# One more gate chunk by seven products in front of the attention, and GpSimd's adds in pairs

## The chip, the cores and the metric

The kernel runs on one core of a Trainium2 chip. The metric is the device time of one execution in microseconds (us); the times of several runs are given as their median. The core has TensorE (PE, with its weight loads as PEld), VectorE (DVE), ScalarE (ACT), GpSimd (POOL) and SyncE (SP), each with an instruction queue of its own, and DMA queues that SP, ACT and POOL feed.

## What is computed

The reference is two transformer blocks in a row over 512 tokens of width 1024, in float32. The change lies in the first one:

```python
proj = h @ w_in                                   # q_a k_a v_a z_a q_b k_b v_b z_b f g
y_a = stick_breaking(q_a, k_a, v_a); y_a = (y_a * silu(z_a)) @ w_o_sb
y_b = forgetting_attention(q_b, k_b, v_b, cumsum(log_sigmoid(f + b_forget)))
y_b = (y_b * silu(z_b)) @ w_o_fox
gates = sigmoid(g + b_gate)                       # 2048 columns: 1024 for y_a, 1024 for y_b
merged = gates[0] * y_a + gates[1] * y_b
x = rmsnorm(x + gate * (merged @ w_out))
```

The second block (pooling, a recurrent mixer, differential attention, memory attention and a convolutional feed-forward layer of width 2816) follows; its feed-forward weights come into this change through their sums alone.

## The kernel before

Activations lie as columns: 128 partitions by 512 tokens for each tile of 128 features. Every large product is done in three matmuls on float32r parts: a value is split in a "high" part (rounded by ScalarE) and a "low" part (value minus high, by VectorE or GpSimd), and high*high, high*low and low*high are added in PSUM.

Weights come as a stream of 1 MB chunks of 256 columns (two tiles). SyncE loads them into three slots, each as soon as TensorE has used the chunk three before it. ScalarE rounds a chunk (`split_weights`, L1508), GpSimd makes its low half in four pieces (`low_weights`, L3310), and TensorE uses it. All of this is an order written out by hand for each engine's queue.

The first block goes through these stages:

- **Seven products in front** (`EARLY_TILES`, `early_product`). For 11 chunks, each chunk's product with h is done as 2x2 blocks by seven half-size products in place of eight: 84 matmuls of 128x256 a chunk. VectorE makes the sums of weights and the low halves here. Gate chunks 6 and 7 (tiles 12 to 15) are the last two of them; they land in the place of the later `vb` tiles (`GATES_AT`), and are stored to memory and loaded again after the attention.
- **First attention ("a", stick-breaking)**, 16 steps in `stick_step`, with the plain products of `vb` and `zb` between them on TensorE; then **second attention ("b", forgetting)**, 16 steps in `fox_step`, with gate tiles 0 to 7 between them. A step of the second one does, on VectorE, the bias subtraction (L2659), two scalings of the weights of the step before (L2671), and the mask of the next step (L2636); TensorE transposes the scaled weights one step later (L669).
- Gate tiles 8 and 9 go with the last steps, and tiles 10 and 11 follow the attention as plain products: 24 matmuls of 128x512 a tile.
- **Output products** "oa" and "ob" (8 tiles each, 12 matmuls of 128x512 a tile) of the gated attention outputs, whose low halves (`gated_lo`) VectorE makes right behind the attention. VectorE multiplies each tile with its gate (L2693, L2698), adds the two (L2701), ScalarE rounds the sum (`merged_hi`, L1535), VectorE subtracts (`merged_lo`, L2360).
- **The w_out product**, 8 tiles of 24 matmuls, each over the eight `merged` slices in order.

In the shadow of the attention two sets of sums of the feed-forward weights ("up sums" and "down sums") are made in device memory: ScalarE's queue copies a first matrix, and GpSimd's queue adds a second one by accumulating DMAs (`add`: eight for the up sums, then eight for the down sums, 704 KB each, behind chosen weight chunks). ScalarE's `later_copies` then copies these sums on; it is called in the loop over the eight `merged` tiles, and before its first copy it waits for all of those adds:

```python
for m in range(KD):
    act.wait_ge(sem("merged_raw"), m + 1)
    high(merged_hi[m], merged_raw[:, m, :], sem("merged_hi"))
    if m % 2 == 0:
        later_copies(S2, S1, m // 2, 2)   # m == 0: waits for 8 + 8 adds to have landed
    if m % 4 == 3:
        split_weights()
```

Of the kernel before, what the change touches and what calls it, by code (L numbers as in the profile page):

```python
# [7 lines left out]
F32 = mybir.dt.float32  # L8
# [78 lines left out]
EARLY_FIRST = 11  # L87
EARLY_TILES = (("qa", 1), ("ka", 0), ("ka", 1), ("za", 0), ("za", 1), ("qb", 0), ("qb", 1), ("kb", 0), ("kb", 1), ("g", 6), ("g", 7))
EARLY = len(EARLY_TILES)
Z_FIRST, EARLY_G = EARLY_TILES.index(("za", 0)), 12  # L90
EARLY_STEPS = [[(c, f) for c, fs in ((i, (P1, R5)), (i - 1, (Q4, P3)), (i, (R7, P6, P2))) if 0 <= c < EARLY for f in fs]
# [93 lines left out]
def build(nc, x_in, mem_in, params_in, consts_in, ada_in, stream_in, with_f_in, down_in, up_in, out, x2_kept, kx_kept, vx_kept, nF_kept, gates_kept, sums_kept, up_sums):  # L185
    with ExitStack() as ctx:
# [156 lines left out]
        GATES_AT = 10240  # L343
        gates = [at(512 * m if m < EARLY_G else GATES_AT + 512 * (m - EARLY_G), T) for m in range(16)]
        merged_raw, merged_lo = at(16384, 8, T), at_r("merged_low", 16384, 8, T)
# [207 lines left out]
        def early_tile(e, half, side):  # L553
            key, c = EARLY_TILES[e]
            if key == "g":
                return gates[2 * c + half][:, TH * side:TH * (side + 1)]
            to = {"qa": qa, "ka": ka, "za": gated["a"], "qb": qb, "kb": kb}[key]
            return to[:, 2 * c + half, TH * side:TH * (side + 1)]
# [99 lines left out]
        def _(pe):  # L658
# [313 lines left out]
            for i in range(2 * N + LAG + 1):  # L972
                if i == 1:
                    pe.wait_ge(sem("product_moved"), MOVED0)
                if i < N:
                    head_scores("a", i, qa, ka, masks[:, 1, :])
                elif i < 2 * N:
                    head_scores("b", i - N, qb, kb, None)
                n = i - LAG
                if n == N:  # L980
                    side(i)
                if 0 <= n < N:
                    head_turns("a", n, SLOTS_A, sem("stick_w"))
                elif N <= n < 2 * N:
                    head_turns("b", n - N, SLOTS_B, sem("fox_w"))
                if i < 2 * N:
                    if n != N:
                        side(i)
                elif i < 2 * N + LAG:
                    if i == 2 * N:  # L990
                        M.use([0, 1, 2, 3])
                    project("g", 1, KD, h, T, first=SIDE_G + i - 2 * N)
                n = i - LAG - 1
                if 0 <= n < N:
                    head_values("a", n, va)
                elif n >= N:
                    if n == N:
                        for m in range(4):
                            F.wait_out(pe, ("vb", m))
                    head_values("b", n - N, vb)  # L1000
# [475 lines left out]
        def _(act):  # L1476
# [269 lines left out]
            for n, (e, f) in enumerate(EARLY_SEQ):  # L1746
                if n and EARLY_SEQ[n - 1][1] in (P1, P6):
                    early_keep(*EARLY_SEQ[n - 1])
                if f == R7:
                    early_sum_high(e + 1, R5)  # L1750
                    early_split(e + 1)
                    if e == 1:
                        act.wait_ge(sem("nF_ready"), 1)
                        act.dma_start(nF_kept, f_work[0:HEADS, 1, :]).then_inc(sem("nF_stored"), 16)
                    if e - 2 in (Z_FIRST, Z_FIRST + 1):
                        for m in range(2):
                            silu("a", 2 * (e - 2 - Z_FIRST) + m)
                elif f == P2:
                    early_sum_high(e + 1, P6)
                    if e == 0:  # L1760
                        act.wait_ge(sem("keys_kept"), 32)
                    early_sum_high(e, P3)
# [44 lines left out]
            def stick_step(i):  # L1807

                if i == 1:
                    act.wait_ge(sem("product_moved"), MOVED0)  # L1810
                    act.dma_start(gates_kept, at(GATES_AT, 4 * T)).then_inc(sem("keys_kept"), 16)
                if i == 2:
                    act.wait_ge(sem("nF_stored"), 16)
                    act.wait_ge(sem("keys_kept"), 48)
                if i % 2 == 0 and 2 <= i <= N:
# [43 lines left out]
            def fox_step(i):  # L1859
# [15 lines left out]
                if i in (5, 9):  # L1875
                    pair = i // 4 + 1
                    M2.wait_out(act, ("b", NB * (pair - 1) - 1))
                    act.dma_start(nF_bc[pair % 2], nF_kept[2 * pair:2 * pair + 2, :].partition_broadcast(P))\
                        .then_inc(sem(f"nF{pair % 2}_loaded"), 16)
                if i % 2 == 0 and 2 <= i <= N:  # L1880
                    gate_inverse(i // 2 - 1)
# [17 lines left out]
            for m in range(4):  # L1899
                gated_high(4 + m)  # L1900
            act.dma_start(at(GATES_AT, 4 * T), gates_kept).then_inc(sem("keys_kept"), 16)
            for m in range(SIDE_G, EARLY_G):
                gate_out(m)
                gate_inverse(m)
            act.wait_ge(sem("keys_kept"), 64)
            for m in range(EARLY_G, 16):
                link(nc.scalar.activation(gates[m], gates[m], ACT.Exp, scale=-1.0, bias=npar("b_gate", m)))
                inverse(gates[m]).then_inc(sem("gates"), 1)

            for _ in range(2):  # L1910
                split_weights()
            for m in range(KD):
# [423 lines left out]
        def _(dve):  # L2336
# [167 lines left out]
            def early_out(n):  # L2504
# [6 lines left out]
                o = early_bank(e, f)  # L2511
                if f == P2:
                    early_moves(stt(early_tile(e, 0, 0), o, by, k1, ALU.mult, ALU.add))
                    if e < EARLY - 1:
# [115 lines left out]


            def mask_block(i):

                b = block_of("b", i)
                v = nF_bc[i // NB % 2][:, :, P * b:P * (b + 1)]
                tt(v, v, con("mask_incl").unsqueeze(1).broadcast_to([P, 2, P]), ALU.add).then_inc(sem("block_masked"), 1)  # L2636

            def fox_step(i):
# [6 lines left out]
                if i < N:  # L2645
# [11 lines left out]
                    for hh in range(2):  # L2657
# [3 lines left out]
                                                             small[:, c:c + 1])  # L2661
                    ins.then_inc(M2.out(("b", i)), 1)
                n = i - 1
                if 0 <= n < N:
# [20 lines left out]

            for m in range(8):
                dve.wait_ge(sem("gated_hi"), m + 1)
                low(gated_lo[:, m, :], gated_raw[:, m, :], gated_hi[m], sem("gated_split"))

# [608 lines left out]
        def _(pool):  # L3298
# [44 lines left out]
            for c in range(4, 8):  # L3343
                low_weights(vb + 5 + c, vb + 6 + c)
                add(S1, A22, 2, c)
                add(S3, A11, 2, c)
            low_weights(vb + 13, mixers + 1)
            with_sums(mixers + 1, mixers + HI, S2, A11, 3, 0)
# [178 lines left out]
def lay_stream(a):  # L3527
# [3 lines left out]
    for i in (2, 0, 1, 3, 4, 5, 6, 7):  # L3531
        columns_ = lay_chunks(w_in[:, 512 * i:512 * (i + 1)], 256)
        parts.append(columns_[::-1] if i == 2 else columns_)
        if i == 5:
            parts.append(by_gates[EARLY_G // 2:])
    parts.append(by_gates[:EARLY_G // 2])
    parts.append(lay_chunks(np.asarray(a["w_o_sb"])[0], 512))
# [61 lines left out]
```

## Time and profile before

| | |
|---|---|
| time, median of 3 runs | 1241.11 us (1240.2 to 1241.29) |
| the profiled execution | 1237.92 us, its span 1236.1 us |
| granted TensorE clock | 1.000 |
| TensorE busy | 1211.6 us, 98% of the span |
| VectorE, ScalarE, GpSimd busy | 855.9, 653.7, 429.7 us |

The span is the time from the first to the last instruction of the profiled execution. Matmuls overlap in the engine, so a busy TensorE is not one at its peak. All times in the rows below count from the start of that span.

### The profile page before, as it was taken

The numbers are of one execution on the slowest core, as the hardware profiler recorded it, in microseconds if no ns is written. First come the engines' busy times: TensorE is split into PE (matmuls) and PEld (weight loads), VectorE is DVE, ScalarE is ACT, GpSimd is POOL, SyncE is SP. The second block draws the span as 40 slices with busy tenths as digits, with TensorE's granted clock in tenths as the row PEclk, the third lists the DMA queues.
The fourth block names the chain that finished last, engine by engine and source line by source line (L and its number), as shares of the span: only waits on it lengthen the run. The fifth ranks groups of instructions, "written<-read, shape, count | busy, mean of one in ns | idle before, by whom it ended". The sixth has DMA issues, their size and how long they took to land.

```text
span 1236.1 us, 22894 instructions
## 1 busy us (share of the span) xinstructions
PE 1211.6 (98%) x9270; PEld 1039.7 (84%) x9270; DVE 855.9 (69%) x1342; ACT 653.7 (53%) x1028; POOL 429.7 (35%) x330
## 2 busy tenths in 40 slices
PE   6999999999999999999998999999999999999999
PEld 5798999876767888777787768788878999999999
DVE  4299897789653275596647758356568888878974
ACT  6555463777765534463456554454335555556452
POOL 5562000422333745455343035540555223333000
PEclk9999999999999999999999999999999999999999
DMA  9953332666976974766321018851533555556554
GB/s 388 362 187 139 117 110 96 241 220 215 265 202 165 251 271 172 238 152 156 92 104 37 4 69 312 258 136 34 143 123 101 164 183 186 187 171 211 187 187 141
DMA packets 42182, 215.53 MB, mean 174 GB/s; under 512 B 5080, under 2 KB 5208, under 8 KB 28128
## 3 DMA queue, kind: packets, MB, share of 16 engines
q1 hardware_dynamic: 34272, 140.74, 32.1%
q0 software_dynamic: 4608, 28.31, 12.1%
q10 hardware_dynamic: 3200, 45.04, 9.7%
q8 instruction: 74, 1.21, 0.4%
q14 instruction: 28, 0.23, 0.1%
HBM read 206.72 MB, written 63.98 MB: 219 GB/s over the span
## 4 chain that ended last, share of the span: by engine, by line
PE 85%; DVE 9%; ACT 3%; issue 2%; POOL 1%; DMA 0%; ACTq 0%; SPq 0%; DVEq 0%; POOLq 0%
PE banks L662 83%; PE banks L669 2%; DVE arena L2619 1%; DVE arena L2616 1%; DVE arena L2621 1%; DVE h_low L2360 1%; ACT weights_high L1508 0%; DMA arena<-in_mem 0%; POOL arena L3369 0%; DVE arena L2450 0%; DVE weights_low L2360 0%; ACT arena L1562 0%; DVE sums L2356 0%; DVE gact_low L2360 0%; DVE arena L3261 0%
## 5 line engine op out<-in xcount | busy, mean ns | idle before, releaser
L3310 POOL TENSOR_TENSOR weights_low<-weights,weights_high 128x512 fp32r<-128x512 f32 (+1 forms) x216 | 309.2, 1460 | 495.7 <-ACT weights_high L1508 495.7
L662 PE MATMUL banks<-h_high_low,weights_high 128*128 128x512 f32 (+1 forms) x696 | 243.5, 350 | 0.4 <-DVE h_low L2360 0.3
L662 PE MATMUL banks<-h_high_low,weights_low 128*128 128x512 f32 (+1 forms) x696 | 236.1, 339 | 0.0
L662 PE MATMUL banks<-h_low,weights_high 128*128 128x512 f32 (+1 forms) x696 | 236.1, 339 | 0.0
L1508 ACT ACTIVATE weights_high<-weights 128x2048 fp32r<-128x2048 f32 (+2 forms) x86 | 127.0, 1489 | 63.6 <-PE banks L662 58.4
L662 PEld LDWEIGHTS banks<-h_high_low,weights_high 128*128 128x128 f32 x696 | 131.3, 189 | 19.3 <-issue 3.0
L662 PEld LDWEIGHTS banks<-h_low,weights_high 128*128 128x128 f32 x696 | 131.3, 189 | 16.5 <-issue 2.4
L662 PEld LDWEIGHTS banks<-h_high_low,weights_low 128*128 128x128 f32 x696 | 131.2, 189 | 16.0
L662 PE MATMUL banks<-arena 64*64 64x64 f32 (+6 forms) x1800 | 116.7, 263 | 1.4 <-POOL arena L3369 0.7
L662 PEld LDWEIGHTS banks<-arena 64*64 64x64 f32 (+3 forms) x1800 | 85.0, 147 | 23.8 <-issue 16.7
L3388 POOL TENSOR_TENSOR weights_low<-weights,weights_high 128x512 fp32r<-128x512 f32 x32 | 48.5, 1537 | 112.6 <-ACT weights_high L1520 112.6
L1520 ACT ACTIVATE weights_high<-weights 128x1024 fp32r<-128x1024 f32 x56 | 59.0, 1057 | 35.2 <-PE banks L662 34.1
L2360 DVE TENSOR_TENSOR weights_low<-weights,weights_high 128x1024 fp32r<-128x1024 f32 (+1 forms) x47 | 60.5, 1287 | 13.9 <-ACT weights_high L1520 11.8
L1562 ACT ACTIVATE arena<-banks 128x512 f32<-128x512 f32 (+4 forms) x78 | 39.3, 513 | 37.8 <-PE banks L669 32.3
L1545 ACT ACTIVATE sums<-xres 128x512 f32<-128x512 f32 x32 | 20.2, 632 | 69.4 <-DVE xres L2713 38.5
L662 PE MATMUL banks<-weights_high,h_high_low 128*128 128x256 f32 (+1 forms) x192 | 55.5, 289 | 0.8 <-POOL weights_low L3310 0.6
L662 PE MATMUL banks<-token_sum_high,weights_low 128*128 128x256 f32 x192 | 54.3, 283 | 0.0
L662 PE MATMUL banks<-weights_high,h_low 128*128 128x256 f32 (+1 forms) x192 | 54.3, 283 | 0.0
L662 PE MATMUL banks<-weights_low,h_high_low 128*128 128x256 f32 (+1 forms) x192 | 54.3, 283 | 0.0
L662 PE MATMUL banks<-token_sum_low,weights_high 128*128 128x256 f32 x192 | 54.2, 282 | 0.0
L662 PE MATMUL banks<-token_sum_high,weights_high 128*128 128x256 f32 x192 | 54.0, 281 | 0.0
L662 PE MATMUL banks<-t_high,weights_low 128*128 128x256 f32 x187 | 52.6, 281 | 0.0
(463 smaller groups left out, 3288.1 us busy)
## 6 DMA issues: line engine op xcount, KB each, us to landing
weights<-in_stream SPq DMA_DIRECT2D x66, 1024.0 KB, 6.0
up_sums<-in_up POOLq DMA_DIRECT2D x16, 1024.0 KB, 9.6
weights<-up_sums SPq DMA_DIRECT2D x64, 256.0 KB, 2.8
weights<-in_up SPq DMA_DIRECT2D x48, 256.0 KB, 2.9
sums_kept<-in_down POOLq DMA_DIRECT2D x16, 704.0 KB, 7.4
arena<-in_ada SPq DMA_DIRECT2D x8, 1024.0 KB, 12.1
weights<-sums_kept SPq DMA_DIRECT2D x9, 704.0 KB, 4.1
sums_kept<-in_down ACTq DMA_DIRECT2D x8, 704.0 KB, 5.9
```

The costliest lines, as they stand in the source:

```text
L662: ins = nc.tensor.matmul(o, lhsT, rhs, start=start, stop=stop, skip_group_check=skip)
L669: ins = nc.tensor.transpose(o, i, ident[0:rows, 0:rows])
L1508: nc.scalar.activation(hi_of(c)[:, cols], raw_of(c)[:, cols], ACT.Copy)\
L1520: nc.scalar.activation(pair_hi(q), pair_raw(q), ACT.Copy).then_inc(sem("piece_hi"), 1)
L1545: nc.scalar.activation(SQ[n][i % 2][:, 0:width], src[:, k, 0:width], ACT.Square)\
L1562: nc.scalar.activation(dst, s_, ACT.Copy).then_inc(ring_.out(key), 1)
L2360: return tt(lo, raw, hi.bitcast(F32), ALU.subtract).then_inc(done, 1)
L2616: link(stt(w, o[:, :, 0:end], 0.0, w, ALU.max, ALU.add))
L2619: ins = nc.vector.tensor_tensor_scan(v, ones(end), v, 0.0, ALU.mult, ALU.add)
L2621: tt(w, o[:, :, 0:end], w, ALU.subtract).then_inc(M2.out(("a", i)), 1)
L3310: nc.gpsimd.tensor_tensor(lo_of(c)[:, cols], raw_of(c)[:, cols], hi_of(c)[:, cols].bitcast(F32), ALU.subtract).then_inc(sem("weights_split ...
L3388: nc.gpsimd.tensor_tensor(piece_of(pair_lo, n), piece_of(pair_raw, n), piece_of(pair_hi, n).bitcast(F32), ALU.subtract).then_inc(sem("piec ...
```

## The change

- `EARLY_TILES` gets a twelfth chunk, gate chunk 5 (tiles 10 and 11), after the `za` chunks. Its result lands at 8192, the place of the later `kb` tiles; ScalarE's queue stores it to `gates_kept` two chunks later, VectorE waits for that store before it writes the first `kb` chunk, and ScalarE's queue loads it to tiles 10 and 11 in step 4 of the second attention.
- Tiles 12 to 15 are copied to the SBUF tile `sums` in place of device memory, and ScalarE's exponentials read them there; the reload after the attention goes.
- The plain products of tiles 10 and 11 go, so "oa" follows the attention directly. The first four subtractions for `gated_lo` (`gated_split`) move into steps 5, 9, 13 and 17 of the second attention. One of ScalarE's chunk splits moves between the exponentials of tiles 13 and 14.
- TensorE waits for the last of the early moves at step 2 of the first attention in place of step 1, and tiles 8 and 9 take banks 2 and 3 first.
- GpSimd's adds to the down sums go four behind one chunk and four behind the next ("oa"'s two) in place of two behind each of four. The adds to the up sums stay behind the same steps.

```diff
-EARLY_TILES = (("qa", 1), ("ka", 0), ("ka", 1), ("za", 0), ("za", 1), ("qb", 0), ... ("g", 6), ("g", 7))
+EARLY_TILES = (("qa", 1), ("ka", 0), ("ka", 1), ("za", 0), ("za", 1), ("g", 5), ("qb", 0), ("qb", 1),
+               ("kb", 0), ("kb", 1), ("g", 6), ("g", 7))
-Z_FIRST, EARLY_G = EARLY_TILES.index(("za", 0)), 12
+Z_FIRST, EARLY_G = EARLY_TILES.index(("za", 0)), 10
...
+        early_gates = {5: at(8192, 2, T), 6: at(GATES_AT, 2, T), 7: at(GATES_AT + 2 * T, 2, T)}
...
             for i in range(2 * N + LAG + 1):                       # TensorE, attention
-                if i == 1:
+                if i == LAG:
                     pe.wait_ge(sem("product_moved"), MOVED0)
...
                     if i == 2 * N:
-                        M.use([0, 1, 2, 3])
+                        M.use([2, 3, 0, 1])
                     project("g", 1, KD, h, T, first=SIDE_G + i - 2 * N)
...
                     early_split(e + 1)                             # ScalarE, early stage
+                    if e >= 2 and EARLY_TILES[e - 2] == ("g", 5):
+                        act.wait_ge(sem("product_moved"), early_moved(e - 2, C12))
+                        act.dma_start(gates_kept, at(8192, 2 * T)).then_inc(sem("keys_kept"), 16)
...
                 if i == 1:                                         # ScalarE, first attention
                     act.wait_ge(sem("product_moved"), MOVED0)
-                    act.dma_start(gates_kept, at(GATES_AT, 4 * T)).then_inc(sem("keys_kept"), 16)
+                    act.dma_start(sums.rearrange("p a b -> p (a b)"), at(GATES_AT, 4 * T)).then_inc(sem("keys_kept"), 16)
                 if i == 2:
                     act.wait_ge(sem("nF_stored"), 16)
-                    act.wait_ge(sem("keys_kept"), 48)
+                    act.wait_ge(sem("keys_kept"), 64)
...
+                if i == 4:                                         # ScalarE, second attention
+                    act.dma_start(at(512 * EARLY_G, 2 * T), gates_kept).then_inc(sem("keys_kept"), 16)
...
-            act.dma_start(at(GATES_AT, 4 * T), gates_kept).then_inc(sem("keys_kept"), 16)
             for m in range(SIDE_G, EARLY_G):
                 gate_out(m)
                 gate_inverse(m)
-            act.wait_ge(sem("keys_kept"), 64)
+            act.wait_ge(sem("keys_kept"), 80)
             for m in range(EARLY_G, 16):
-                link(nc.scalar.activation(gates[m], gates[m], ACT.Exp, scale=-1.0, bias=npar("b_gate", m)))
+                if m == 14:
+                    split_weights()
+                src = gates[m] if m < 12 else sums[:, m - 12, :]
+                link(nc.scalar.activation(gates[m], src, ACT.Exp, scale=-1.0, bias=npar("b_gate", m)))
                 inverse(gates[m]).then_inc(sem("gates"), 1)
-            for _ in range(2):
-                split_weights()
+            split_weights()
...
                 if f == P2:                                        # VectorE, early stage
+                    if EARLY_TILES[e] == ("kb", 0):
+                        dve.wait_ge(sem("keys_kept"), 48)
...
+            def gated_split(m):
+                dve.wait_ge(sem("gated_hi"), m + 1)
+                low(gated_lo[:, m, :], gated_raw[:, m, :], gated_hi[m], sem("gated_split"))
...
                     ins.then_inc(M2.out(("b", i)), 1)              # VectorE, fox_step, after L2659
+                if i % 4 == 1 and 5 <= i <= N + 1:
+                    gated_split(i // 4 - 1)
                 n = i - 1
...
-            for m in range(8):
-                dve.wait_ge(sem("gated_hi"), m + 1)
-                low(gated_lo[:, m, :], gated_raw[:, m, :], gated_hi[m], sem("gated_split"))
+            for m in range(4, 8):
+                gated_split(m)
...
             for c in range(4, 8):                                  # GpSimd, adds to the down sums
-                low_weights(vb + 5 + c, vb + 6 + c)
+                if c % 2 == 0:
+                    low_weights(vb + 7 + c // 2, vb + 8 + c // 2)
                 add(S1, A22, 2, c)
                 add(S3, A11, 2, c)
-            low_weights(vb + 13, mixers + 1)
+            low_weights(vb + 11, mixers + 1)
```

The order of the chunks in the stream is changed to match, and `gates_kept` shrinks to two tiles.

## Rows read from the trace of the kernel before

**Rows 1.** The page, part 1: busy us (share), instructions.

```profile
PE 1211.6 (98%) x9270; PEld 1039.7 (84%) x9270; DVE 855.9 (69%) x1342; ACT 653.7 (53%) x1028; POOL 429.7 (35%) x330
```

**Rows 2.** Windows of TensorE: us, PE busy (x), PEclk, DMA share, GB/s.

```profile
111.75:221.83 110.08, 109.99 (x927) 1.00 0.31 110
394.77:406.13 11.36, 11.36 (x51) 1.00 1.00 290
406.13:450.92 44.79, 44.79 (x193) 1.00 0.92 262
```

**Rows 3.** Waits of TensorE, 205 to 330 us: total, times, longest.

```profile
PE banks L662 <- DVE arena L2621: 0.2, 1, 0.2
PE banks L669 <- ACT arena L1831: 0.2, 1, 0.2
```

**Rows 4.** Waits of TensorE, 330 to 520 us.

```profile
PE banks L662 <- DVE h_low L2360: 0.3, 1, 0.3
```

**Rows 5.** Timeline of ScalarE, step 2 of the first attention: start, us, what.

```profile
229.69 0.60 ACT L1562 ACTIVATE arena<-banks 128x512 f32<-128x512 f32 x1 [1.81 <-DMA gates_kept<-arena]
```

**Rows 6.** Timeline of VectorE, GpSimd and TensorE, step 5 of the second attention.

```profile
327.79 0.56 DVE L2659 CUSTOM_DVE_ANT_0 arena<-banks,arena 128x384 f32<-128x384 f32 x1
328.05 5.56 POOL L3310 TENSOR_TENSOR weights_low<-weights,weights_high 128x512 fp32r<-128x512 f32 x4 [13.17 <-ACT weights_high L1508]
...
328.47 2.59 DVE L2671 TENSOR_SCALAR arena<-arena,small 128x512 f32<-128x512 f32 x2
...
332.19 0.66 PE L669 MATMUL banks<-consts,arena 128*128 128x128 f32 x4
```

**Rows 7.** Timeline of VectorE, step 9 of the second attention.

```profile
348.23 2.59 DVE L2671 TENSOR_SCALAR arena<-arena,small 128x512 f32<-128x512 f32 x2
```

**Rows 8.** Timeline of VectorE in the merged loop.

```profile
432.25 1.64 DVE L2701 TENSOR_TENSOR arena<-arena 128x512 f32<-128x512 f32 x1
...
439.95 0.69 DVE L2360 TENSOR_TENSOR merged_low<-arena,merged_high_a 128x512 fp32r<-128x512 f32 x1 [1.18 <-ACT merged_high_a L1535]
...
441.89 0.69 DVE L2360 TENSOR_TENSOR merged_low<-arena,merged_high_a 128x512 fp32r<-128x512 f32 x1
...
452.95 1.47 DVE L2360 TENSOR_TENSOR merged_low<-arena,merged_high_b 128x512 fp32r<-128x512 f32 x2
```

**Rows 9.** Timeline of ScalarE around its first later copy (ACTq: its sequencer issues).

```profile
433.93 0.64 ACT L1535 ACTIVATE merged_high_a<-arena 128x512 fp32r<-128x512 f32 x1 [3.20 <-DVE arena L2701]
438.74 0.50 ACTq L1769 DMA_DIRECT2D up_sums<-up_sums  x1
439.29 0.63 ACT L1535 ACTIVATE merged_high_a<-arena 128x512 fp32r<-128x512 f32 x1 [4.73 <-DVE arena L2701]
```

**Rows 10.** Timeline of GpSimd: two of its four pairs of adds.

```profile
392.36 1.65 POOL L3328 DMA_DIRECT2D sums_kept<-in_down  x2
...
406.94 1.62 POOL L3328 DMA_DIRECT2D sums_kept<-in_down  x2
```

**Rows 11.** DMA, 392 to 409 us: busy tenths in 40 equal slices.

```profile
DMA  0000929689999999899998999999999998305867
```

**Rows 12.** DMA queues, 412 to 420 us: packets, MB, share (software_dynamic: GpSimd's).

```profile
q0 software_dynamic: 327, 1.66, 103.2%
```

**Rows 13.** DMA queues, 422 to 427 us (q1: SyncE's loads).

```profile
q0 software_dynamic: 109, 0.59, 58.4%
q1 hardware_dynamic: 113, 0.91, 45.9%
```

**Rows 14.** DMA queues, 400 to 405 us (q10: ScalarE's, here the reload).

```profile
q0 software_dynamic: 76, 0.43, 41.8%
q1 hardware_dynamic: 78, 0.64, 31.6%
q10 hardware_dynamic: 78, 0.64, 30.1%
```

**Rows 15.** DMA queues, 407.6 to 410.6 us.

```profile
q1 hardware_dynamic: 114, 0.93, 92.1%
```

More of the change, by code:

```diff
@@ L87 @@
 EARLY_FIRST = 11
-EARLY_TILES = (("qa", 1), ("ka", 0), ("ka", 1), ("za", 0), ("za", 1), ("qb", 0), ("qb", 1), ("kb", 0), ("kb", 1), ("g", 6), ("g", 7))
+EARLY_TILES = (("qa", 1), ("ka", 0), ("ka", 1), ("za", 0), ("za", 1), ("g", 5), ("qb", 0), ("qb", 1),
+               ("kb", 0), ("kb", 1), ("g", 6), ("g", 7))
 EARLY = len(EARLY_TILES)
-Z_FIRST, EARLY_G = EARLY_TILES.index(("za", 0)), 12
+Z_FIRST, EARLY_G = EARLY_TILES.index(("za", 0)), 10
 EARLY_STEPS = [[(c, f) for c, fs in ((i, (P1, R5)), (i - 1, (Q4, P3)), (i, (R7, P6, P2))) if 0 <= c < EARLY for f in fs]
@@ L343, in build @@
         GATES_AT = 10240
-        gates = [at(512 * m if m < EARLY_G else GATES_AT + 512 * (m - EARLY_G), T) for m in range(16)]
+        gates = [at(512 * m if m < 12 else GATES_AT + 512 * (m - 12), T) for m in range(16)]
+        early_gates = {5: at(8192, 2, T), 6: at(GATES_AT, 2, T), 7: at(GATES_AT + 2 * T, 2, T)}
         merged_raw, merged_lo = at(16384, 8, T), at_r("merged_low", 16384, 8, T)
@@ L555, in early_tile @@
             if key == "g":
-                return gates[2 * c + half][:, TH * side:TH * (side + 1)]
+                return early_gates[c][:, half, TH * side:TH * (side + 1)]
             to = {"qa": qa, "ka": ka, "za": gated["a"], "qb": qb, "kb": kb}[key]
@@ L3534, in lay_stream @@
         if i == 5:
-            parts.append(by_gates[EARLY_G // 2:])
-    parts.append(by_gates[:EARLY_G // 2])
+            parts.append(by_gates[6:])
+        if i == 3:
+            parts.append(by_gates[5:6])
+    parts.append(by_gates[:5])
     parts.append(lay_chunks(np.asarray(a["w_o_sb"])[0], 512))
@@ L3591 @@
     nF_kept = nc.dram_tensor("nF_kept", [HEADS, T], F32, kind="Internal").ap()
-    gates_kept = nc.dram_tensor("gates_kept", [P, 4 * T], F32, kind="Internal").ap()
+    gates_kept = nc.dram_tensor("gates_kept", [P, 2 * T], F32, kind="Internal").ap()
     sums_kept = nc.dram_tensor("sums_kept", [4, DOWN_PAIRS, P, DOWN_W], F32, kind="Internal").ap()
```

## Prediction

> **What bounds the kernel now.** I read the page's busy shares first, then TensorE's waits, then the stretches around the places that the diff touches. TensorE is busy for 98% of the span [rows 1], at a granted clock of 1.00 in every stretch read here [rows 2]. Its named waits add up to 0.4 us between 205 and 330 us and to 0.3 us between 330 and 520 us [rows 3, 4]. So in the first block a microsecond of TensorE work saved is a microsecond of time, unless the other engines then come too late; the rest of this text is about whether they do. Times below are those of the profile; G is 394.77, where gate tile 10 starts now and the output products "oa" would start afterwards.
>
> **TensorE's work.** The seven-product stretch takes 110.08 us for 11 chunks, a wait of a quarter microsecond included, so 10.0 a chunk; tiles 10 and 11 take 11.36 us as plain products [rows 2]. About 0.1 us of the 11.36 is the switch from the attention's short matmuls, which "oa" inherits. The trade is 10.0 for 11.3: minus 1.3 us. Its lower bound is the same, since both prices are measured; DVE's and ScalarE's share of a twelfth chunk lies beside these products, as it does for the eleven.
>
> **What the early chunk brings on ScalarE's and SyncE's queues.** SyncE issues the same loads in the same places relative to the chunks. ScalarE issues a store of tiles 10 and 11 in the early stage, a reload in step 4 of the second attention, and no reload after it; each issue is a third of a microsecond beside TensorE-bound work. I cost them at nothing; without that cover they would be 0.3 us each. `i == LAG` for `i == 1` and the bank order [2, 3, 0, 1] remove waits of which the trace shows none at those places: nothing.
>
> **The copy into `sums`.** In step 2 ScalarE waits for the old store of the four tiles and then drains bank 7 at 229.69 and goes on [rows 5]; TensorE's 0.2 us waits come from the chain that starts there [rows 3]. Now the 1 MB goes from SBUF to SBUF. The trace has no such copy. If it lands sooner, some of the 0.4 us of waits is won; if it took two microseconds more, the chain and TensorE would lose about those two. I take 0, because the amount and the source are the old ones.
>
> The Trainium skill (DMA: Bandwidth & Descriptors, "Where 436 GB/s comes from") lets SBUF-to-SBUF traffic run at 435 GB/s against about 358 with HBM at one end. By it the copy would land some 0.5 us sooner (an estimate from that page) and the sum would be up to 0.4 us lower; no run here shows it.
>
> **Four DVE subtractions move into the second attention.** `gated_split` runs in steps 5, 9, 13 and 17, between the subtraction of the biases (L2659) and the two scalings (L2671) that release TensorE's transposes. In step 5 GpSimd starts its first weight piece at 328.05, before L2659 is done at 328.35; its four pieces take 5.56 us. Meanwhile each DVE instruction with SBUF operands alone lasts until the running piece is over: the two scalings take 2.59 us together. The scalings end at 331.06 and the transposes start at 332.19 [rows 6], a slack of 1.13 us. Steps 9 and 13 repeat this to the hundredth; step 9's scalings stand in [rows 7]. One more two-operand subtraction of 512 columns costs 1.5 to 1.8 us in that company (L2701 at 432.25 took 1.64 [rows 8]), so the transposes wait 0.4 to 0.7 us; I take 0.6. In step 17 nothing is waiting behind it. Three times 0.6 is plus 1.8 us. Bounds: 0, if DVE gets there before the first piece (0.69 us, inside the slack), and 2.1.
>
> The Trainium skill (SBUF — State Buffer, "SBUF: two separate sides") calls the port pair of DVE and GpSimd an exclusive lock that whoever starts first holds for its whole instruction. By it everything hangs on the 0.22 us by which GpSimd's first piece is ahead: were DVE first, the term would be 0. The rows show GpSimd first in all three steps, and I follow them.
>
> **GpSimd's adds and ScalarE's wait for them.** This is the largest term. Removing tiles 10 and 11 moves "oa", "ob" and the w_out product 11.3 us towards the attention. `later_copies`, unchanged, still makes ScalarE wait after its first `merged_hi` until all eight adds to the down sums have landed. Now ScalarE finishes that first rounding at 434.57, is held, and issues the copy at 438.74 [rows 9]. Behind it in its queue stand the other seven roundings of merged and the splits of w_out's first two chunks; DVE's `merged_lo` waits for the roundings (1.18 us at 439.95 [rows 8]), GpSimd for the splits, TensorE for both. It costs nothing today, as w_out starts at 450.92 [rows 2], needs the eighth slice 21 matmuls later (4.9 us) at 455.8, and DVE delivers it at 454.42 [rows 8].
>
> Afterwards w_out starts at G + 44.8 (four chunks of "oa" and "ob" in 44.79 us [rows 2]) and needs the eighth slice at G + 49.7. From the release to the eighth slice: 1.2 us to the second rounding [rows 9], 0.7 for its subtraction, then five tiles of product, sum and subtraction at 1.95 each (439.95 to 441.89 [rows 8]), 9.7; GpSimd's split of w_out's first chunk falls into it and stretches three or four of these by 1.0 (1.64 for 0.69 [rows 8]), 3.3; last rounding and subtraction 1.3. Sum 16.1. So the adds have to land by G + 33.6.
>
> When do they land? GpSimd issues the first two at 392.36, as before, and the other two of that batch 1.6 us later; the second batch follows the low half of the next chunk, at 406.94 [rows 10]. Two issues take 1.65 us, so a batch takes 3.3 us in front of the next low half, which waits for ScalarE anyway: hidden. What counts is the transfers. The first bytes move at 393.7 [rows 11]. Alone the adds move 1.66 MB in 8 us, 0.207 MB/us [rows 12]; beside one chunk load 0.59 MB in 5 us, while the load moves 0.91 [rows 13]; beside a load and the old reload 0.43 MB, while those move 1.28 [rows 14]. Between 407.6 and 410.6 only a load moves [rows 15]: the queue of adds had run dry at about 407 [rows 11], and the second pair had yet to start. The new order removes this pause of 3.6 us and the reload.
>
> Eight adds are 5.77 MB (704 KB each). Three chunk loads (1.05 MB, 5.8 us each) fall beside them and take 17.3 us, in which the adds move 2.04 MB; the other 3.73 MB take 18.0 us. From 393.7 that ends at 429.0. The same sum for the kernel before is 8.2 us beside two transfers (0.70 MB), the pause, 11.6 us beside two loads (1.37 MB) and 17.9 us alone: 41.3 us, to 435.0, where the release was at 438.74, 3.7 later. Scaled to the shorter sum that is 3.2 more: 432, which is G + 37.2 and 3.6 us after the point above. I take plus 3.3 us, since the stretching of DVE's instructions is the chain's least certain part. Bounds: with the plain sum it is 0.6 us; with adds that meet no load (27.9 us in all) it is 0; with a landing at G + 39 it is 5.2.
>
> The Trainium skill (DMA: Bandwidth & Descriptors, "Anatomy of one DMA — SWDGE (gpsimd) path") gives about 2 us plus the bytes over 436 GB/s for one such DMA. By it the eight adds would be done near G + 20 (an estimate from that page) and this term would be 0. The accumulating adds of [rows 12] move at less than half that rate, so the row decides.
>
> **Sum.** Minus 1.3, plus 1.8, plus 3.3: plus 3.8 us. On the profiled execution's 1237.92 that gives 1241.7. That execution lies 3.2 below the median of the runs shown, 1241.11, which becomes 1244.9.
>
> **Rivals.** 0.2% (2.5 us) is about what a measurement of this kernel can tell from no change.
>
> A (forecast): both stalls come, 1244.9, with bounds of its own from 1242.3 to 1247.8. Chance 0.46.
>
> B: the adds are late, but DVE wins the port first in steps 5, 9 and 13, or its order hides it: minus 1.3 plus 3.3, 1243.1. For it speaks that 0.22 us decides; against it, that all three steps show the same lead. Chance 0.14.
>
> C: the transposes wait, but the adds land by G + 33.6, as four in the queue move faster than two or the loads overlap less: minus 1.3 plus 1.8, 1241.6. For it: the plain sum, G + 34.2, is 0.6 us from that point. Against it: the same sum falls 3.7 us short on the kernel before. Chance 0.14.
>
> D, the other side: the change gives just what its products save, since the early adds land by G + 33.6 and the subtractions fit their slack. Then it is minus 1.3, 1239.8, or 1239.1 with the waits of [rows 3, 4] gone. It decides at the landing of the last add. Chance 0.26.
>
> Slower by over 0.2%: nearly all of A and under half of B, 0.50. Faster by over 0.2%: only the low end of D with scatter, 0.05. Within: 0.45. The range 1239.0 to 1247.8 reaches from D's low end to A's upper bound and leaves out a little at both sides.
>
> **What would show it.** Right: the early stage 10.0 us longer and no plain tiles behind the attention; gaps of half a microsecond on TensorE before the transposes behind steps 5, 9 and 13, with L2671 ending 1.7 us later; ScalarE idle for about 9 us after the first rounding of merged, released by the last add near G + 37; TensorE waiting some 3 us inside w_out's first tile. Wrong: a release before G + 33.6, L2671's end unmoved, or a copy into `sums` that holds ScalarE in step 2 for more than the old store's time.

## The result, and the profile after

The changed kernel takes 1244.67 us (median of 8 runs, 1241.14 to 1247.26), the kernel before 1240.01 in the same comparison (8 runs): a ratio of 1.0047, with a 95% interval from 1.0036 to 1.0059. The forecast was 1244.9 and slower. In a second comparison the same kernel gave 1.0037 (1.0024 to 1.0050). The time was met within 0.3 us, and part of that is luck. The change itself measured 4.7 us (1244.67 less 1240.01) where 3.8 was forecast, on a kernel before that is 1.1 us faster in this comparison than the 1241.11 that the forecast started from; and of the terms of the sum one was left out, and two were too large, by about as much together.

The profiled execution took 1244.3 us, with a span of 1241.4 (before: 1237.92 and 1236.1). First the page's busy shares, then windows of TensorE, whose columns are those of [rows 2]: the early stage, the four chunks of "oa" and "ob", and the head of w_out.

```profile
PE 1212.7 (98%) x9306; PEld 1041.6 (84%) x9306; DVE 864.0 (70%) x1356; ACT 656.9 (53%) x1034; POOL 424.7 (34%) x326
```

```profile
112.56:232.53 119.97, 119.88 (x1011) 1.00 0.33 114
...
408.98:453.88 44.90, 44.90 (x194) 1.00 1.04 287
453.88:464.00 10.12, 8.48 (x36) 1.00 0.65 229
```

The window of the early stage above closes 0.07 us short of the attention's first matmul, at 232.60; up to there the stage grew from 110.08 us [rows 2] to 120.04: 10.0 for a chunk that took 11.36 as plain products. The four output chunks take 44.90 us, as before. What is new is in front of them and behind them: the attention, from the end of the early stage to the first output product, takes 176.4 us (232.60 to 408.98), where it took 172.9 (221.83 to 394.77, [rows 2]), and in the 10.12 us behind 453.88 TensorE is busy for only 8.48.

The view of waits names the two places. TensorE's waits from 330 to 395 us, and from 395 to 520 us (total, times, longest):

```profile
PE banks L671 <- DVE arena L2688: 3.1, 3, 2.1
```

```profile
PE banks L664 <- DVE merged_low L2368: 1.6, 2, 1.1
PE banks L664 <- DVE h_low L2368: 0.3, 1, 0.3
```

Against [rows 4] two lines are new. L671 and L2688 are the transposes and the scalings of the second attention, L669 and L2671 before; `merged_low` is what the first tile of w_out reads. The bill of this one execution, from its windows and the starts of its matmuls: the first chunk 0.8 us later than before, which is taken for chance (over the changed kernel's and the experiments' profiles it lies between 0.8 earlier and 1.2 later); products 10.0 less 11.36; attention plus 3.4 (its three waits, 3.1, and a tenth around each); w_out's first tile plus 2.2, of which 1.6 are named waits; 0.3 spread over the rest. Sum 5.3, which is the difference of the spans.

**The adds and ScalarE's hold.** ScalarE's timeline in the merged loop, beside [rows 9]; the last three lines are the fifth, the sixth and the seventh of the eight roundings:

```profile
436.88 0.63 ACT L1537 ACTIVATE merged_high_a<-arena 128x512 fp32r<-128x512 f32 x1 [3.20 <-DVE arena L2717]
445.36 0.48 ACTq L1774 DMA_DIRECT2D up_sums<-up_sums  x1
445.89 0.63 ACT L1537 ACTIVATE merged_high_a<-arena 128x512 fp32r<-128x512 f32 x1 [8.37 <-DMA sums_kept<-in_down]
...
450.95 0.61 ACT L1537 ACTIVATE merged_high_b<-arena 128x512 fp32r<-128x512 f32 x1
453.00 0.63 ACT L1537 ACTIVATE merged_high_b<-arena 128x512 fp32r<-128x512 f32 x1 [1.43 <-DVE arena L2717]
456.41 0.63 ACT L1537 ACTIVATE merged_high_b<-arena 128x512 fp32r<-128x512 f32 x1 [2.78 <-DVE arena L2717]
```

TensorE's timeline in w_out's first tile:

```profile
457.15 0.40 PE L664 MATMUL banks<-merged_high_b,weights_low 128*128 128x512 f32 x1
458.13 0.50 PE L664 MATMUL banks<-merged_high_b,weights_high 128*128 128x512 f32 x1 [0.59 <-DVE merged_low L2368]
...
458.70 0.40 PE L664 MATMUL banks<-merged_high_b,weights_low 128*128 128x512 f32 x1
460.15 0.48 PE L664 MATMUL banks<-merged_high_b,weights_high 128*128 128x512 f32 x1 [1.05 <-DVE merged_low L2368]
```

The profile puts the 8.37 us before the second rounding down to the adds. ScalarE issues its copy at 445.36, which is 36.4 us after the output products begin (408.98). Then the chain runs as it stands in the prediction, and TensorE waits for the sixth and the seventh slice.

**A wait that was not foreseen.** VectorE, GpSimd and TensorE around step 8 of the second attention, and in front of them ScalarE's issues; in brackets the idle time before an instruction and what ended it:

```profile
335.04 0.33 ACTq L1886 DMA_DIRECT2D arena<-gates_kept  x1
337.21 0.50 ACTq L1777 DMA_DIRECT2D sums_kept<-in_down  x1
339.12 0.33 ACTq L1883 DMA_DIRECT2D forget_rows<-nF_kept  x1
```

```profile
357.75 0.43 DVE L2651 TENSOR_TENSOR forget_rows<-forget_rows,consts 128x256 f32<-128x256 f32 x1 [8.80 <-DMA forget_rows<-nF_kept]
...
360.31 0.44 PE L671 MATMUL banks<-consts,arena 128*128 128x128 f32 x2 [2.08 <-DVE arena L2688]
...
361.73 0.69 DVE L2368 TENSOR_TENSOR gated_low<-arena,gated_high_a 128x512 fp32r<-128x512 f32 x1
...
363.44 2.69 POOL L3326 TENSOR_TENSOR weights_low<-weights,weights_high 128x512 fp32r<-128x512 f32 x2 [17.25 <-ACT weights_high L1510]
```

The forget rows (for a pair of heads, the sums of the forget gates' logarithms that L2659 subtracts, copied to all 128 partitions) that step 8 needs are issued at 339.12 and used at 357.75. The view of DMA gives the time from issue to landing; before, and after:

```profile
forget_rows<-nF_kept ACTq DMA_DIRECT2D x1, 512.0 KB, 10.0
```

```profile
arena<-gates_kept ACTq DMA_DIRECT2D x1, 512.0 KB, 13.2
forget_rows<-nF_kept ACTq DMA_DIRECT2D x1, 512.0 KB, 18.6
```

The reload of tiles 10 and 11, which the change moved to step 4, is issued 4.1 us ahead of them on the same queue. So VectorE sits idle for 8.80 us, and the transposes of step 8 wait 2.08. In step 9, as a consequence, VectorE reaches its subtraction of gated (361.73, 0.69 us) before GpSimd starts its pieces (363.44), and no wait follows. In step 5 it is the other way round:

```profile
338.76 5.81 POOL L3326 TENSOR_TENSOR weights_low<-weights,weights_high 128x512 fp32r<-128x512 f32 x4 [13.18 <-ACT weights_high L1510]
338.99 1.61 DVE L2368 TENSOR_TENSOR gated_low<-arena,gated_high_a 128x512 fp32r<-128x512 f32 x1
...
340.71 2.74 DVE L2688 TENSOR_SCALAR arena<-arena,small 128x512 f32<-128x512 f32 x2
...
343.50 1.09 PE L671 MATMUL banks<-consts,arena 128*128 128x128 f32 x8 [0.53 <-DVE arena L2688]
```

### The profile page after: what moved, and what is told of

The parts are those of the page before. It is cut to its first block, busy times and chain, and to the rows that moved or that the text cites. A ratio compares the mean times of both kernels' runs of the same rounds, so it can differ in the third digit from the quotient of the medians.

```text
span 1241.4 us, 23003 instructions
## 1 busy us (share of the span) xinstructions
PE 1212.7 (98%) x9306; PEld 1041.6 (84%) x9306; DVE 864.0 (70%) x1356; ACT 656.9 (53%) x1034; POOL 424.7 (34%) x326
## 4 chain that ended last, share of the span: by engine, by line
PE 79%; DVE 10%; ACT 4%; DMA 2%; issue 2%; POOL 1%; ACTq 0%; DVEq 0%; SPq 0%; POOLq 0%
PE banks L664 78%; PE banks L671 2%; DMA sums_kept<-in_down 2%; DVE arena L2629 1%; POOL weights_low L3326 1%; ACT weights_high L1510 1%; DVE arena L2626 1%; DVE arena L2631 1%; DVE arena L2688 1%; DVE h_low L2368 1%; DVE merged_low L2368 0%; DVE weights_low L2368 0%; POOL arena L3386 0%; DMA arena<-in_mem 0%; DVE arena L2674 0%
## 5 line engine op out<-in xcount | busy, mean ns | idle before, releaser
L3326 POOL TENSOR_TENSOR weights_low<-weights,weights_high 128x512 fp32r<-128x512 f32 (+1 forms) x212 | 303.9, 1464 | 504.9 <-ACT weights_high L1510 504.9
L664 PE MATMUL banks<-h_high_low,weights_high 128*128 128x256 f32 (+1 forms) x688 | 239.1, 348 | 0.4 <-DVE h_low L2368 0.3
L664 PE MATMUL banks<-h_low,weights_high 128*128 128x256 f32 (+1 forms) x688 | 231.7, 337 | 0.0
L664 PE MATMUL banks<-h_high_low,weights_low 128*128 128x256 f32 (+1 forms) x688 | 231.6, 337 | 0.0
L664 PEld LDWEIGHTS banks<-h_high_low,weights_low 128*128 128x128 f32 x688 | 129.6, 188 | 15.4
```

Source lines behind the costliest of these rows:

```text
L664: ins = nc.tensor.matmul(o, lhsT, rhs, start=start, stop=stop, skip_group_check=skip)
L3326: nc.gpsimd.tensor_tensor(lo_of(c)[:, cols], raw_of(c)[:, cols], hi_of(c)[:, cols].bitcast(F32), ALU.subtract).then_inc(sem("weights_split ...
```

## Experiments

All ratios are to the kernel before, on one chip within a comparison, with 95% intervals; the first four experiments share one comparison, the last four another.

**The reload later.**

```diff
-                if i == 4:
+                if i == 10:
                     act.dma_start(at(512 * EARLY_G, 2 * T), gates_kept).then_inc(sem("keys_kept"), 16)
```

> The changed kernel with one edit: ScalarE issues the reload of gate tiles 10 and 11 in step 10 of the second attention, behind its last load of forget rows, and no longer in step 4. Theory: the reload of half a megabyte in front of them in ScalarE's queue made the forget rows land 18.6 us after their issue (10.0 before the change), so VectorE started step 8 late and TensorE waited 2.1 us. Then they land within 12 us, the 2.1 us wait is gone, step 9's transposes get the wait of 0.5 us that steps 5 and 13 have, and the kernel takes 1.6 us less than the changed one: ratio to the kernel before about 1.0034. Rival: the copies, adds and weight loads that share the DMA engines at that time make the rows late; then they still land more than 16 us after their issue, the wait of about 2 us stays, and the ratio stays at 1.0047.

Ratio 1.0043 (1.0028 to 1.0059). TensorE's waits from 330 to 398 us, and the landing of the forget rows:

```profile
PE banks L671 <- DVE arena L2688: 1.6, 3, 0.5
```

```profile
forget_rows<-nF_kept ACTq DMA_DIRECT2D x1, 512.0 KB, 12.7
```

Three waits of 0.5 us, in steps 5, 9 and 13, where there were two and one of 2.1; the rows land in 12.7 us, so the rival's 16 is ruled out. That is 1.5 us less of waits (1.7 by the length of the attention). The time decides nothing: its interval holds the expected 1.0034 and the rival's 1.0047. Where the saving went in the profiled execution, the windows from w_out's first tile on say, with one from the second block as the last:

```profile
454.00:456.00 2.00, 1.48 (x7) 0.86 (x5) 2.00 (x3) 0.63 (x1) 1.42 (x1) 1.00 0.87 266
456.00:458.00 2.00, 0.96 (x3) 0.48 (x3) 1.87 (x4) 0.67 (x2) 0.00 (x0) 1.00 1.77 741
458.00:460.00 2.00, 1.95 (x5) 1.59 (x6) 0.69 (x1) 1.96 (x2) 0.16 (x1) 0.56 0.09 33
460.00:462.00 2.00, 2.00 (x6) 1.54 (x6) 1.08 (x2) 0.33 (x1) 2.00 (x2) 0.58 0.00 0
...
680.00:686.00 6.00, 6.00 (x122) 4.34 (x125) 3.61 (x8) 3.45 (x9) 0.00 (x0) 0.72 0.01 3
```

The columns are the length, the busy time of PE, PEld, DVE, ACT and POOL, then the granted clock, the DMA share and GB/s. After the waits (1.48 and 0.96 us busy of 2.00) the granted clock is 0.56 and 0.58 for 4 us, near the lower level, 1.2 GHz: w_out's third tile starts 14.9 us after its first, in the changed kernel 13.4, so 1.5 us are lost there, about as much as the edit saved. Five or six matmuls fit into 2 us there, ten or eleven right behind, at 1.00. In the changed kernel's profile the clock stays at 1.00 at this place. The second fall, 0.72 from 680 to 686 us, in a stretch of short matmuls of the second block, cost about 1.3 more against the changed kernel, so this execution's span, 1242.1 us, is even 0.7 longer than that one's. So it is settled by the trace that the reload in step 4 makes the wait in step 8, while a gain in time was not shown. Whether the reload delays the rows by its place on their queue, or its half megabyte would do so from any queue, was not tried.

**The subtraction behind the scalings.**

```diff
-                if i % 4 == 1 and 5 <= i <= N + 1:
-                    gated_split(i // 4 - 1)
                 n = i - 1
                 if 0 <= n < N:
...
                     ins.then_inc(sem("fox_w"), 1)
+                if i % 4 == 1 and 5 <= i <= N + 1:
+                    gated_split(i // 4 - 1)
```

> The changed kernel with one edit: in steps 5, 9, 13 and 17 the subtraction of gated stands behind the two scalings on VectorE, not in front of them. Theory: its 1.6 us in front of the scalings is what delays the transposes of steps 5 and 13 by 0.5 us each; behind them nobody waits for it. Then TensorE's two waits of 0.5 us are gone, the one of 2.1 us in step 8 stays, and the kernel takes 1.0 us less than the changed one: ratio to before about 1.0039. Rival: the subtraction only shifts the delay, to the mask and the biases of the next step, as all of them wait for GpSimd's pieces; then a wait of about 0.5 us stands one step later, and the ratio stays at 1.0047.

Ratio 1.0044 (1.0027 to 1.0061); the profiled execution took 1240.59 us, but the six runs spread from 1240.23 to 1247.06, so the time can't tell the two theories apart. The waits can. TensorE, 330 to 398 us, and step 5 on VectorE and TensorE:

```profile
PE banks L671 <- DVE arena L2686: 1.1, 1, 1.1
```

```profile
338.75 2.59 DVE L2686 TENSOR_SCALAR arena<-arena,small 128x512 f32<-128x512 f32 x2
...
341.26 1.75 DVE L2368 TENSOR_TENSOR gated_low<-arena,gated_high_a 128x512 fp32r<-128x512 f32 x1
...
342.47 1.09 PE L671 MATMUL banks<-consts,arena 128*128 128x128 f32 x8
```

The scalings take 2.59 us as in [rows 6], the transposes wait for nothing, and the subtraction still takes 1.75, with nobody behind it. Only step 8's wait is left (1.1 us here, the rows landed 17.0 us after their issue). No wait stands one step later: the rival is wrong.

**ScalarE's hold behind five roundings.**

```diff
-                if m % 2 == 0:
-                    later_copies(S2, S1, m // 2, 2)
+                if m >= 4:
+                    later_copies(S2, S1, m - 4, 2)
```

> The changed kernel with one edit: ScalarE issues the four later copies of the up sums behind its roundings 4, 5, 6 and 7 of merged, not behind 0, 2, 4 and 6, so that its wait for the eight adds stands behind five roundings. Theory: the hold from the first rounding to the landing of the last add is what makes TensorE wait in the first tile of w_out. Then ScalarE is not idle for 8 us, the waits of 1.6 us there are gone, and with them the rest of what that stretch lost: 1.6 to 2.2 us less than the changed kernel, ratio to before 1.0029 to 1.0034. Rival: the chain of product, sum, rounding and subtraction on VectorE, stretched by GpSimd's pieces, is late by itself; then TensorE still waits 1 us or more there, and the ratio is 1.004 or more.

Ratio 1.0030 (1.0011 to 1.0050), the expected 1.0029 to 1.0034, but the interval holds the rival's 1.004 too; the waits decide. ScalarE's wait for the adds now stands behind five roundings, and TensorE's waits for `merged_low` are gone:

```profile
PE banks L671 <- DVE arena L2688: 2.6, 3, 1.6
```

```profile
PE banks L664 <- DVE h_low L2368: 0.3, 1, 0.3
```

These are TensorE's only waits from 330 to 398 and from 398 to 520 us. So it was the hold, not the chain on VectorE by itself.

**The adds spread as before.**

```diff
             for c in range(4, 8):
-                if c % 2 == 0:
-                    low_weights(vb + 7 + c // 2, vb + 8 + c // 2)
+                low_weights(vb + 5 + c, vb + 6 + c)
                 add(S1, A22, 2, c)
                 add(S3, A11, 2, c)
-            low_weights(vb + 11, mixers + 1)
+            low_weights(vb + 13, mixers + 1)
```

> The changed kernel with one edit: GpSimd's adds to the down sums are spread again, two behind the low half of each of four chunks, the first two at the same place. Theory: the landing of the last add sets ScalarE's release, and every microsecond of it beyond about 34 us after the start of the output products is a microsecond of TensorE in the first tile of w_out. The last two are then issued some 23 us later than the last four of the changed kernel and land about 44 us after that start, not 36: 7 to 8 us more than the changed kernel, ratio to before about 1.011. Rival: the adds are bound by their transfers, and spreading the issues changes nothing; then the last lands at about 36 and the ratio stays at 1.0047.

Ratio 1.0126 (1.0112 to 1.0141). ScalarE's hold, and TensorE's waits from 398 to 520 us:

```profile
450.78 0.48 ACTq L1774 DMA_DIRECT2D up_sums<-up_sums  x1
451.31 0.63 ACT L1537 ACTIVATE merged_high_a<-arena 128x512 fp32r<-128x512 f32 x1 [16.57 <-DMA sums_kept<-in_down]
```

```profile
PE banks L664 <- DVE arena L2714: 4.9, 1, 4.9
PE banks L664 <- DVE merged_low L2368: 2.3, 2, 1.3
PE banks L664 <- DVE h_low L2368: 0.3, 1, 0.3
```

The release comes 44.6 us after the start of the output products (450.78, from 406.20), 8.2 later than in the changed kernel, and TensorE waits 7.2 us instead of 1.6. (The last two adds are issued 30.2 us after that start, the changed kernel's last four from 12.2 on: 18 us later, not the expected 23.) Here VectorE, which waits for a rounding, does not even get to the products of "ob" in time (L2714, 4.9 us). The granted clock falls here too; the window of TensorE, with the columns of [rows 2]:

```profile
455.00:458.00 3.00, 3.00 (x10) 0.65 1.35 481
```

With that, the way from the first output product to the second tile of w_out is 8.2 us longer than in the changed kernel, as much as the landing is later. Of it 5.6 us are named waits, and the fallen clock is in the rest; so the run does not show that a microsecond of landing costs a microsecond by itself. The ratio lies just above the expected 1.011. The pairs, which look like a mere rearrangement, keep the change from costing more than twice as much.

**The three edits together.** The diff is that of the first three experiments.

> The changed kernel with the three edits together: the reload of tiles 10 and 11 in step 10, the subtraction of gated behind the scalings, the later copies behind roundings 4 to 7. Theory: the change's products are worth 1.3 us (10.0 for 11.36), and all of its loss lies in the three waits that these edits remove, so that what is left is the gain: no wait of TensorE over 0.3 us between 330 and 500 us, 1.3 us less than the kernel before, ratio 0.999, and a granted clock of 1.00 behind the attention. Rival: something besides these waits is lost (DMA traffic that moved, later chunks whose splits come late); then the ratio is 1.000 or more though these waits are gone.

Ratio 0.9994 (0.9985 to 1.0003): medians 1238.36 against 1239.21, 0.85 us less, which this measurement can't tell from no change. The trace is clearer. From 330 to 500 us the view of waits has no line at all. From the first matmul on the early sums to the first product of w_out it takes 336.3 us, where it took 337.7 before: 1.3 us less, which is what the products were to gain. 1.2 of that was lost in the second block in this execution:

```profile
774.07 5.87 POOL L3326 TENSOR_TENSOR weights_low<-weights,weights_high 128x512 fp32r<-128x512 f32 x4 [1.39 <-ACT weights_high L1510]
774.54 1.76 DVE L2368 TENSOR_TENSOR h_low<-h,h_high_low 128x512 fp32r<-128x512 f32 x1
...
776.35 0.50 PE L664 MATMUL banks<-h_high_low,weights_high 128*128 128x512 f32 x1 [1.18 <-DVE h_low L2368]
```

The subtraction of h, which took 0.68 us in the kernel before and was done ahead of GpSimd's pieces, started 0.47 us behind GpSimd here and took 1.76. The same wait, of 1.5 and 1.6 us, stands in the profiles of the third and fourth experiments, and in none of the other five that hold the whole change. What puts the two engines in one order or the other there was not tried.

**All eight subtractions behind the attention.**

```diff
-                if i % 4 == 1 and 5 <= i <= N + 1:
-                    gated_split(i // 4 - 1)
...
-            for m in range(4, 8):
+            for m in range(8):
                 gated_split(m)
```

> The kernel with the three edits together, but with all eight subtractions of gated behind the attention, where the kernel before has them. Theory: there the plain products of tiles 10 and 11 covered them; now the first output products follow at once and need the low part of gated's first tile in their second matmul, so TensorE waits 1.5 to 2.5 us at the start of the output products: 0.0012 to 0.002 over the ratio of the kernel with three edits, about 1.001. Rival: VectorE is idle enough at the end of the attention to have them ready; then no such wait, and the two ratios agree.

Ratio 1.0000 (0.9988 to 1.0011), 0.0006 over the one with three edits: smaller than expected, and not told from it by the time. The wait is there, once, at the first output product:

```profile
PE banks L664 <- DVE gated_low L2368: 1.5, 1, 1.5
```

So, by the trace, the move into the attention pays: left behind it, the subtractions cost TensorE 1.5 us, about what the products gain.

**The kernel before with the subtractions moved, and nothing else.** The diff adds `gated_split` to the kernel before, in the place where the change has it.

> The kernel before with one part of the change alone: the four subtractions of gated in steps 5, 9, 13 and 17 of the second attention, in front of the scalings. Theory: GpSimd starts its pieces ahead of VectorE in all of steps 5, 9 and 13 there, so the transposes wait 0.5 us in each: 1.6 us of waits, ratio 1.0013. Rival: as in the changed kernel's step 9, VectorE gets its subtraction in first in some of them; then fewer than three waits, and a ratio within 0.0005 of 1.

Ratio 1.0020 (1.0006 to 1.0034). TensorE's waits from 328 to 398 us:

```profile
PE banks L669 <- DVE arena L2678: 1.6, 3, 0.5
```

Three waits in three steps: with the forget rows in time, GpSimd is first in each.

**The changed kernel once more.**

> The changed kernel itself, once more, beside the others on their chip. Theory: its waits stand in the same places and are not chance: 0.5 us in steps 5 and 13, 1 to 2.2 us in step 8 behind the late forget rows, none in step 9, 1.6 us of named waits in the first tile of w_out; ratio 1.0047 within 0.0015. Rival: the late forget rows are chance of one execution; then step 8 shows no wait, step 9 shows one of 0.5 us instead, and the ratio is nearer 1.003.

Ratio 1.0037 (1.0024 to 1.0050). TensorE's waits, 328 to 398 and 398 to 520 us:

```profile
PE banks L671 <- DVE arena L2688: 2.5, 3, 1.4
```

```profile
PE banks L664 <- DVE merged_low L2368: 1.4, 2, 1.0
PE banks L664 <- DVE h_low L2368: 0.3, 1, 0.3
```

The same places. In step 8 the wait is 1.4 us instead of 2.1, so its size varies between executions; that the rows are late does not (18.6, 18.0, 18.1, 17.4 and 17.0 us in the five profiles with the reload in step 4; 12.7, 12.1 and 12.8 in the three with it in step 10; 10.0 and 13.4 in the two of the kernel before, with no reload there).

## Why the prediction was right, and where it was not

**Products, minus 1.3.** Right. The early stage grew by 10.0 us for 11.36, minus 1.4; its wait of a quarter microsecond stands in both kernels (0.37 us between two starts of matmuls, at 218.43 before and at 229.20 after). With the stalls edited away the stretch up to w_out is 1.3 us shorter in the profile, which the times neither confirm nor exclude.

**The copy into `sums`, 0.** Right. It landed in 4.8 us where the store took 6.0, and ScalarE doesn't wait for it, but TensorE's two waits of 0.2 us are still there (the same two lines as [rows 3]), so nothing was won by it. The Trainium skill (DMA: Bandwidth & Descriptors, "Where 436 GB/s comes from") lets such a copy be faster; the trace agrees in direction, by 1.2 us where the estimate was 0.5.

**The reload in step 4, costed at nothing.** This step failed. The prediction said of ScalarE's new issues that "each issue is a third of a microsecond beside TensorE-bound work" and priced the issue alone. What it left out is the transfer behind it on that queue: with half a megabyte in front of them the forget rows landed 18.6 us after their issue instead of 10.0, and TensorE lost 2.1 us in step 8 (1.4 in the second profile). Taking the reload out of the way and nothing else removed the wait.

**The subtractions in steps 5, 9 and 13, plus 1.8.** The mechanism was right, the sum too large by 0.7. A step costs 0.53 us rather than 0.6, and step 9 cost nothing, because the late forget rows had turned the order of the two engines round. Where they are in time, all three steps pay (1.6 us in two experiments). The Trainium skill (SBUF — State Buffer, "SBUF: two separate sides") says that whichever of DVE and GpSimd starts first holds their shared port for its whole instruction; the trace agrees, with 1.61 us for the subtraction behind GpSimd's start and 0.69 for the same one ahead of it.

**The late adds, plus 3.3.** Right in its cause, and too large by 1.1 us. ScalarE was held as forecast, for 8 us, and the release came 36.4 us after the start of the output products against 37.2. From there it took 15.4 us to the eighth subtracted slice, not 16.1 (the prediction's own terms add up to 16.2). The slice that TensorE waited for last was the seventh, 14.7 us behind the release; its matmuls begin 4.2 us into w_out (18 matmuls), not 4.9. By these numbers 36.4 + 14.7 is 2.0 us past 44.9 + 4.2, about the measured loss of 2.2.

**The sum.** Forecast minus 1.3, plus 1.8, plus 3.3. By the trace minus 1.4, plus 1.1 (and 0.3 around all three waits of the attention), plus 2.1 for the rows, plus 2.2 for w_out: about plus 4.2 up to the second tile of w_out, and 0.3 in small steps elsewhere. The forecast of plus 3.8 is near the measured 4.7 because the reload's 2.1 us, left out, took the place of 1.8 that two terms had too much: that is luck. The upper end of the range, 1247.8, is not what the prediction's bounds give (minus 1.3, plus 2.1, plus 5.2 on 1241.1 is 1247.1, and a landing at G + 39 is 5.4 past G + 33.6, not 5.2); the measured time lies below all of these. Rival A, both stalls, is what happened, with a third beside them. B is excluded by the waits in steps 5 and 13, C and D by the release at 36.4.

## What to carry to other kernels

A DMA that is moved can have two prices: its issue, and what stands behind it on its queue. List the next transfers of that queue and when each is needed; here a reload that nobody was waiting for cost more than the gain of the whole change. When work in the middle is removed, everything that hid behind it comes due earlier: a hold that lay behind 11 us of plain products became a stall, and moving the wait behind the work that does not need it was a two-line cure. Small subtractions between a busy GpSimd and a waiting TensorE belong behind the instruction that TensorE waits for, not in front of it.

## What the runs showed of the hardware that was not expected

TensorE's granted clock fell after waits of about a microsecond in a dense stretch: 0.56 and 0.58 over 4 us in the first experiment, behind two stretches in which TensorE was busy for 1.48 and 0.96 us of 2.00, and 0.65 in the fourth. It doesn't fall each time; the changed kernel's own profile has 1.00 there with the same waits. Over whole executions the kernel with all three waits removed had a mean clock of 1.000 in 10 of 11 runs, the one with only the reload moved 0.997 or less in 4 of 6, and the one with the adds spread 0.994 to 0.999 in all 4. But what decides is not shown: with a wait of 1.5 us at the first output product (the subtractions behind the attention) all 11 runs had 1.000, and the third experiment, which has no waits in w_out, 0.997 to 0.999 in 3 of 8. So a stall can cost more than its own length, as the 1.5 us in the first experiment did beside waits of 1.6, and when it does stays open.

The other is how little decides between two orders of VectorE and GpSimd: leads of a quarter to a half of a microsecond (0.23 us in step 5, 0.47 in the second block) turn a subtraction of 0.7 us into one of 1.6 to 1.8.
